# An encoder layer on one core: modulation rows by DMA, ring slots reordered, first two tiles together, three weight loads ahead

## The chip, the core and the metric

One core of one Trainium2 chip runs the whole layer. The time is that of one execution on the device, in microseconds; smaller is better. The engines are TensorE (PE, with its weight loads as PEld), VectorE (DVE), ScalarE (ACT), GpSimd (POOL) and SyncE (SP), which issues most of the DMAs.

## The reference, cut to what matters

One layer over x of 512 tokens by 1024 channels, all in float32. The part that the change touches is the first lines:

```python
mod = silu(c) @ w_ada + b_ada                     # (1, 6 * 1024)
sh1, sc1, gt1, sh2, sc2, gt2 = split(mod, 6)
h = rmsnorm(x, norm_mix_pre) * (1.0 + sc1) + sh1
z = h @ w_in                                      # (512, 1024) @ (1024, 4864)
zc, zr, zg = split(z, [1024, 1024 + 1792])        # conv, rwkv, gate columns
u = zc[:, :512] * sigmoid(zc[:, 512:])            # then a causal 31-tap depthwise convolution
...
zr = zr + (shifted(zr) - zr) * mu                 # then lora products, the RWKV-7 recurrence, heads normed
y = (g_conv * (silu(ln(conv)) @ p_conv) + g_rwkv * (rwkv @ p_rwkv)) @ w_o
x = x + gt1 * rmsnorm(y, norm_mix_post)
... a mixture of 64 experts follows, under sh2, sc2 and gt2
```

## The kernel before, in words

The kernel is a row of stages, each a block in which every engine runs its own written-out list of instructions; semaphores tie the lists together, and no planner moves anything. `project` makes mod and z, `rwkv` the recurrence, `merge_route` joins the two branches and chooses the experts, `experts` and `combine` do the rest.

`project` streams its weights through a ring of three slots of 2 MB (`ring`), in the order of the list STREAM: the 12 column slices of w_ada ("ada", 512 columns each) and the 10 slices of w_in ("in"). SyncE issues each load when the item three places before it in that list is done with: for an ada slice this is its sum on TensorE (s_adam), for an in slice the last z tile made from it (s_z).

An ada slice i becomes one row of mod, spread over all 128 partitions, in this way. VectorE sums silu(c)[k] times the eight 128-row pieces of the slice into `ada_acc` (`ada_partial`, L459, one instruction a piece, each waiting for the one before). For the first four slices TensorE takes two of the eight pieces itself (`ada_direct`, DIRECT = 2). TensorE then adds over the partitions with a matmul by ones (`ada_sum`, L373) and adds the bias row with a second matmul, by a column of the identity against `wide`, the 20 rows of b_ada and of the four norm gains (L374). Where the row is a scale or a gate, a third matmul (`gain_row`, L354) spreads the gain's row, ScalarE copies it to mod (`gain_copy`, L297), and VectorE multiplies it in (`mod_row`, L474). Slices 0 to 3 give sh1 and sc1, which h needs, and so come before h; slices 4 to 11 are used in later stages only, and are made one by one between the z tiles: the partial after the first tile of in slice s (VectorE), the three matmuls after its fourth tile (TensorE), for s from 1 to 8.

z comes in 38 tiles of 128 columns by 512 tokens. The product is made from exact halves: ScalarE rounds a pair of tiles' weights to `w_hi` (`split`, L310), GpSimd subtracts that from the weights into `ring_lo` (L269), h likewise is h_hi (ScalarE, L315) and h_lo (VectorE, L494 and L497), and a tile is 24 matmuls (L429), three for each of eight pieces k. Three PSUM banks rotate: ScalarE takes each tile, and for the 14 rwkv tiles VectorE adds the shifted part (L519) before the bank is free. Tiles 0 to 7 are the conv columns, 8 to 19 rwkv, 20 to 35 gates, 36 and 37 rwkv again. From tile 9 on VectorE also makes the 124 taps of the convolution (L506 and L510), six behind a tile, on the tiles that aren't the first of their slice.

`rwkv` begins with loads of the lora weights w2, a2 and g2 (L673 to L675) and with the products from them (L882). `merge_route` begins with loads of p_conv and p_rwkv and others (L1389 on); GpSimd writes `headones`, a block matrix of ones by head (L1421), TensorE takes head means with it (L1528), and goes on with p_conv (L1546).

## Time and profile before

| | us |
|---|---|
| median of 3 runs | 1486.5 |
| lowest, highest | 1485.4, 1490.94 |
| the profiled execution's own time | 1488.43 |
| span in its profile | 1486.7 |
| TensorE busy in the span | 1351.9 (91%) |
| VectorE busy | 1046.8 (70%) |
| ScalarE busy | 613.1 (41%) |
| GpSimd busy | 347.0 (23%) |

Time in the profile is counted from the span's start. `project` covers about the first 305 us of it, `rwkv` the time to 501.5, the merge and the routing the time to about 700, the experts nearly all of the rest. A count behind a row (x7) says that neighbouring instructions of one line are merged; the bracket at a row's end is the idle time ahead of it on its engine and what ended it. A float32 matmul by `ones` or `headones` is counted as two. PEclk is the granted TensorE clock as a share of full speed, 2.4 GHz.

### The profile page before, as it was taken

To read this page: it belongs to the slowest core of one execution; us is meant where nothing else is said; L and a number is where in the kernel's file an instruction comes from. 1 tells how busy PE (TensorE), PEld (TensorE's weight loads), DVE (VectorE), ACT (ScalarE), POOL (GpSimd) and SP (SyncE) were. 2 spreads that over 40 slices of the span, in tenths; PEclk is the share of its full clock that TensorE was granted. 3 is DMA by queue.
4 is the path that set the end of the run, shared out by engine and by line. 5 is a ranking of instruction groups with operands and counts; after the bars stand their busy time and mean duration, and the time that the engine had idled before them with its cause. 6 is when DMAs were issued, how large, how long until landed. Compare 5 with 4: busy or idle time off the path is not lost. (4 is left out here: it accounts for less than half of the span.)

```text
span 1486.7 us, 18817 instructions
## 1 busy us (share of the span) xinstructions
PE 1351.9 (91%) x5795; PEld 926.4 (62%) x5795; DVE 1046.8 (70%) x1651; ACT 613.1 (41%) x931; POOL 347.0 (23%) x350
## 2 busy tenths in 40 slices
PE   5799999974889799996899999999999999999947
PEld 3577677632779444443676776767767677676713
DVE  4539999968753253363688888888888888888617
ACT  3322212134224211212465655656656566565502
POOL 0243424233000000001222232322323223232200
PEclk9799999887789899998899999999999999999969
DMA  8434443210000461133599999999999999998358
GB/s 303 153 135 149 177 163 114 85 71 0 2 1 1 193 240 77 64 142 152 222 342 357 344 357 353 359 344 349 376 393 358 347 344 354 355 355 293 133 221 351
DMA packets 85266, 339.26 MB, mean 228 GB/s; under 512 B 16918, under 2 KB 20176, under 8 KB 58084
## 3 DMA queue, kind: packets, MB, share of 16 engines
q1 hardware_dynamic: 65400, 304.97, 54.5%
q0 software_dynamic: 19584, 33.60, 6.2%
q8 instruction: 27, 0.44, 0.1%
q14 instruction: 19, 0.16, 0.0%
q10 hardware_dynamic: 236, 0.09, 0.0%
HBM read 332.31 MB, written 44.04 MB: 253 GB/s over the span
## 5 line engine op out<-in xcount | busy, mean ns | idle before, releaser
L2158 DVE TENSOR_TENSOR gate_up_low<-gate_up,gate_up_high 128x1024 fp32r<-128x1024 f32 x204 | 244.7, 1220 | 42.2 <-ACT gate_up_high L2049 42.2
L2130 PE MATMUL py<-down_ring,hT 128*128 128x512 f32 x544 | 250.0, 602 | 0.9 <-ACT hT L2068 0.9
L2091 PE MATMUL p_gate_up<-gate_up_high,x_hi 128*128 128x512 f32 x544 | 242.7, 446 | 5.3 <-DVE x_lo L2167 5.3
L2091 PE MATMUL p_gate_up<-gate_up_low,x_hi 128*128 128x512 f32 x544 | 217.1, 399 | 0.0
L2091 PE MATMUL p_gate_up<-gate_up_high,x_lo 128*128 128x512 f32 x544 | 215.9, 397 | 0.0
L2049 ACT ACTIVATE gate_up_high<-gate_up 128x1024 fp32r<-128x1024 f32 x204 | 203.7, 1051 | 0.6 <-PEq L1308 0.6
L2130 PEld LDWEIGHTS py<-down_ring,hT 128*128 128x128 f32 x544 | 98.0, 190 | 98.8 <-issue 98.7
L2020 POOL TENSOR_TENSOR carrier<-offsets 1x1 f32<-1x1 f32 x136 | 29.2, 215 | 522.1 <-DVE tokens L2176 475.2
L269 POOL TENSOR_TENSOR ring_lo<-ring,w_hi 128x2048 fp32r<-128x2048 f32 x19 | 91.5, 4814 | 179.3 <-ACT w_hi L310 179.3
L2091 PEld LDWEIGHTS p_gate_up<-gate_up_high,x_hi 128*128 128x128 f32 x544 | 104.1, 191 | 45.1 <-issue 21.4
L429 PE MATMUL pz<-h_hi,w_hi 128*128 128x512 f32 x304 | 123.4, 406 | 7.7 <-DVE h_lo L497 7.7
L2091 PEld LDWEIGHTS p_gate_up<-gate_up_high,x_lo 128*128 128x128 f32 x544 | 103.8, 191 | 29.9 <-issue 10.8
L429 PE MATMUL pz<-h_lo,w_hi 128*128 128x512 f32 x304 | 122.1, 402 | 0.0
L429 PE MATMUL pz<-h_hi,ring_lo 128*128 128x512 f32 x304 | 122.1, 402 | 0.0
L2091 PEld LDWEIGHTS p_gate_up<-gate_up_low,x_hi 128*128 128x128 f32 x544 | 103.0, 189 | 24.2
L2036 POOL DMA_INDIRECT expert_rows<-y,row_ids x68 | 112.9, 1660 | 19.9 <-issue 19.9
L2073 ACT ACTIVATE y<-py 128x512 f32<-128x512 f32 x68 | 40.7, 599 | 179.4 <-PE py L2130 179.4
L510 DVE SCALAR_TENSOR_TENSOR co<-upad,taps,co 128x512 f32<-128x512 f32 x120 | 104.3, 936 | 0.0
L2158 DVE TENSOR_TENSOR gate_up_low<-x_again,gate_up_high 128x1024 fp32r<-128x1024 f32 x68 | 82.5, 1233 | 19.4 <-ACT gate_up_high L2049 19.4
L2062 ACT ACTIVATE x_hi<-px 128x512 fp32r<-128x512 f32 x136 | 73.9, 595 | 41.7 <-PE px L2104 41.7
L2167 DVE TENSOR_TENSOR x_lo<-px,x_hi 128x512 fp32r<-128x512 f32 x136 | 87.1, 682 | 4.1 <-ACT x_hi L2062 4.1
L459 DVE SCALAR_TENSOR_TENSOR ada_acc<-ring,silu_c,ada_acc 128x512 f32<-128x512 f32 x76 | 78.3, 1030 | 2.7
(359 smaller groups left out, 2038.2 us busy)
## 6 DMA issues: line engine op xcount, KB each, us to landing
down_ring<-in_we_down SPq DMA_DIRECT2D x68, 1024.0 KB, 9.6
gate_up<-in_we_gate SPq DMA_DIRECT2D x51, 1024.0 KB, 7.0
gate_up<-in_we_up SPq DMA_DIRECT2D x51, 1024.0 KB, 9.8
ring<-in_w_ada SPq DMA_DIRECT2D x12, 2048.0 KB, 7.9
ring<-in_w_in SPq DMA_DIRECT2D x9, 2048.0 KB, 10.1
x_again<-in_we_gate SPq DMA_DIRECT2D x17, 1024.0 KB, 7.0
x_again<-in_we_up SPq DMA_DIRECT2D x17, 1024.0 KB, 9.8
rows<-expert_rows SPq DMA_DIRECT2D x6, 2048.0 KB, 18.3
```

The source lines that it names most:

```text
L269: pool.tensor_tensor(pair(ring_lo, b), pair(ring, b), exact(w_hi[:, b % 2, :, :]), ALU.subtract).then_inc(s_wlo, 1)
L429: last = pe.matmul(pz[n % 3][:, :], weights, h[:, k, :], start=(k == 0 and i == 0), stop=(k == KD - 1 and i == 2))
L459: last = nc.vector.scalar_tensor_tensor(out=acc[:, i % 2, :], in0=ring[:, slot, k, :], scalar=c_k, in1=acc[:, i % 2, :], op0=ALU.mult, op1 ...
L510: done[r] = link.sign(nc.vector.scalar_tensor_tensor(out=mix.co[:, r, :], in0=u, scalar=tap, in1=mix.co[:, r, :], op0=ALU.mult, op1=ALU.add))
L2036: pool.indirect_dma_start(moe.rows, bass.IndirectOffsetOnAxis(row_ids[:, u % 4, 0:1], 0), y[:, u % 2, :], None, bounds_check=last_row, oob ...
L2049: act.activation(w_hi[:, u % 2, :, piece(i), :], moe.gate_up[u % RING][:, :, piece(i), :], ACT.Copy).then_inc(s_hi, 1)
L2062: act.activation(x_hi[:, u % 2, 4 * half:4 * half + 4, :], px[half][:, :].rearrange("p (k s) -> p k s", k=4), ACT.Copy).then_inc(s_xhi, 1)
L2073: act.activation(y[:, u % 2, 0:N], py[0][:, :], ACT.Copy).then_inc(s_yA, 1)
L2091: mm = pe.matmul(pgu[u % 2][:, :], x[:, u % 2, k, :], weights, start=(k == 0 and n == 0), stop=(k == KD - 1 and n == 2))
L2130: mm = pe.matmul(py[half][:, :], hT[:, u % 2, k, :], weights[:, k, half * N:half * N + N], start=(k == 0), stop=(k == 1))
L2158: V.tensor_tensor(moe.low[u % RING][:, :, piece(i), :], moe.gate_up[u % RING][:, :, piece(i), :], exact(w_hi[:, u % 2, :, piece(i), :]), A ...
L2167: V.tensor_tensor(x_lo[:, u % 2, ks, :], px[half][:, :].rearrange("p (k s) -> p k s", k=4), exact(x_hi[:, u % 2, ks, :]), ALU.subtract).th ...
```

## The change

- `wide` holds only bias rows: four rows of b_ada for slices 0 to 3, loaded by ScalarE's queue, and then a cleared tile of 128 rows (GpSimd's memset, behind the sum of slice 3, and ahead of its first `ring_lo`) into whose row 0 the bias of each slice from 4 on is loaded. VectorE's first piece takes it in, so the sum of these slices is one matmul.
- The gain rows are spread by four DMAs of 512 KB from ScalarE's queue straight into mod; `gain_row` and `gain_copy` go.
- x is the first load of SyncE's queue; c and the bias go by ScalarE's. A slot that held an ada slice is free as soon as VectorE's partial and TensorE's direct pieces have read it, without the sum. STREAM names slots: ada 4, 5 and 6 follow each other in slot 2 behind in 0 and in 1; then in 2, ada 7, in 3, ada 8, in 4, ada 9, in 5, ada 10, in 6, ada 11, in 7, in 8, in 9. in 0 comes in two halves with a semaphore each.
- TensorE takes four pieces of ada 3 (DIRECT = 2, 2, 2, 4) and the order of its work ahead of h changes.
- z tiles 0 and 1 are made together, 48 matmuls, with those of `ring_lo` two pieces behind. The remainder of pair 1 is made by VectorE and not by GpSimd.
- Partials and sums: 4 right before and after tiles 0 and 1; 5 behind tiles 1 and 3; 6 behind tiles 4 and 6; 7 to 11 behind the first and fourth tile of in slices 2 to 6. The taps go on the other tiles from 9, and so end with tile 33, not 35.
- w2, a2 and g2 are loaded into `ada_acc` once all sums are made; `headones` lives through all three stages; p_conv is loaded during `rwkv`, once the last Z64 product is made, and not in the merge.

The diff, cut (left out: names of semaphores, the slices' places in memory, and the same buffer written as `conv_stat` in place of `conv_stat[:, :]`):

```diff
-STREAM = [("ada", i) for i in range(4)]
...
-STREAM_AT = {item: n for n, item in enumerate(STREAM)}
 RING1 = 3
+FIRST, EARLY = 4, 3
+STREAM = ([(("ada", 0), 0), (("ada", 1), 1), (("ada", 2), 2), (("ada", 3), 0), (("in", 0), 1), (("in", 1), 0)]
+          + [(("ada", FIRST + _i), 2) for _i in range(EARLY)])
+for _i in range(2, len(IN_SLICES)):
+    STREAM.append((("in", _i), 1 - _i % 2))
+    if FIRST + EARLY + _i - 2 < ADA:
+        STREAM.append((("ada", FIRST + EARLY + _i - 2), 2))
+SLOT = dict(STREAM)
+USE = {item: sum(s == slot for _, s in STREAM[:_n]) for _n, (item, slot) in enumerate(STREAM)}
+BEFORE_IT = {item: [i for i, s in STREAM[:_n] if s == slot][-1:] for _n, (item, slot) in enumerate(STREAM)}
 PAIR = 2 * P
-FIRST = 4
-DIRECT = 2
+DIRECT = (2, 2, 2, 4)
 Z_TILES = [(s, t) for s, (_, w) in enumerate(IN_SLICES) for t in range(w // P)]
...
             if kind == "ada":
-                engine.wait_ge(s_adam, i + 1)
+                engine.wait_ge(s_ada, i + 1)
+                if i < FIRST:
+                    engine.wait_ge(s_dir, i + 1)
...
+        PARTIAL_AT = {1: FIRST + 1, 4: FIRST + 2}
+        SUM_AFTER = {3: FIRST + 1, 6: FIRST + 2}
+        for i in range(FIRST + EARLY, ADA):
+            PARTIAL_AT[Z_TILES.index((i - FIRST - EARLY + 2, 0))] = i
+            SUM_AFTER[Z_TILES.index((i - FIRST - EARLY + 2, 3))] = i
+        ROW_AT = {n + 1: i for n, i in SUM_AFTER.items()}
...
             sp.dma_start(x[:, :, :], w["x"][0].rearrange("(t p) d -> p t d", p=P)).then_inc(s_x, 16)
...
+            for item, slot in STREAM:
+                kind, i = item
+                for earlier in BEFORE_IT[item]:
+                    free_wait(sp, earlier)
...
-                sp.dma_start(ring[:, n % RING1, :, 0:width],
-                             source[:, at:at + width].rearrange("(k p) n -> p k n", p=P)).then_inc(
-                                 s_slot[n % RING1], 16)
+                parts = ((0, PAIR, s_half), (PAIR, N, s_slot[slot])) if item == ("in", 0) else ((0, width, s_slot[slot]),)
+                for c0, c1, landed in parts:
+                    sp.dma_start(ring[:, slot, :, c0:c1],
+                                 source[:, at + c0:at + c1].rearrange("(k p) n -> p k n", p=P)).then_inc(landed, 16)
+                if kind == "ada" and i >= FIRST:
+                    if i == FIRST:
+                        sp.wait_ge(s_zero, 1)
+                    sp.dma_start(wide[0:1, :], w["b_ada"][0:1, i * N:(i + 1) * N]).then_inc(s_brow, 16)
+            sp.wait_ge(s_adam, ADA)
+            sp.dma_start(acc[0:LORA_W, 0, :], w["w2"][0]).then_inc(mix.s_w, 16)
+            sp.dma_start(acc[LORA_W:P, 0, :], w["a2"][0]).then_inc(mix.s_w, 16)
+            sp.dma_start(acc[:, 1, :], w["g2"][0]).then_inc(mix.s_w, 16)
         @block.gpsimd
...
+            pool.wait_ge(s_adam, FIRST)
+            pool.memset(wide[:, :], 0.0).then_inc(s_zero, 1)
             for b in range(len(Z_TILES) // 2):
+                if b == 1:
+                    continue
...
+            act.dma_start(crow[:, :], w["c"][0].rearrange("(r n) -> r n", n=P)).then_inc(s_crow, 16)
+            act.dma_start(wide[0:FIRST, :], w["b_ada"][0, 0:FIRST * N].rearrange("(r n) -> r n", n=N)).then_inc(s_wide, 16)
+            rows = (keep.mod[:, D:2 * D], keep.mod[:, 2 * D:3 * D], keep.mod[:, 4 * D:5 * D], keep.gate2[:, :])
+            def gain_rows(g):
+                row = w[GAINS[g]][0].rearrange("(a n) -> a n", a=1).to_broadcast([P, D])
+                act.dma_start(rows[g], row).then_inc(s_gains if g else s_gain, 16)
...
-            def gain_copy(i):
-                if has_gain(i):
-                    act.wait_ge(s_gain, gains_to(i) + 1)
-                    act.activation(mod_part(keep, i), pg[:, :], ACT.Copy).then_inc(s_adag, 1)
...
+            gain_rows(0)
...
+            for g in range(1, len(GAINS)):
+                gain_rows(g)
...
+                if b == 0:
+                    act.wait_ge(s_half, 16)
+                else:
+                    slot_wait(act, ("in", Z_TILES[2 * b][0]))
...
-            def gain_row(i):
...
-                    pe.matmul(pg[:, :], keep.ident[0:N_WIDE, row:row + 1].to_broadcast([N_WIDE, P]),
-                              wide[:, :], start=True, stop=True).then_inc(s_gain, 1)
...
+                slot_wait(pe, ("ada", i))
+                for k in range(DIRECT[i]):
+                    mm = pe.matmul(out[:, :], keep.silu_c[:, k:k + 1].to_broadcast([P, P]), ring[:, SLOT[("ada", i)], k, :],
+                                   start=(k == 0), stop=False)
+                mm.then_inc(s_dir, 1)
...
+                mm = pe.matmul(out[:, :], keep.ones[:, :], acc[:, i % 2, :], start=(i >= FIRST), stop=(i >= FIRST))
...
-            def ada_sum(i):
-                out = pm[i % 2]
-                pe.wait_ge(s_ada, i + 1)
-                pe.matmul(out[:, :], keep.ones[:, :], acc[:, i % 2, :], start=(i >= FIRST), stop=False)
-                pe.matmul(out[:, :], keep.ident[0:N_WIDE, i:i + 1].to_broadcast([N_WIDE, P]), wide[:, :],
-                          start=False, stop=True).then_inc(s_adam, 1)
+                    mm = pe.matmul(out[:, :], keep.ident[0:FIRST, i:i + 1].to_broadcast([FIRST, P]), wide[0:FIRST, :],
+                                   start=False, stop=True)
+                mm.then_inc(s_adam, 1)
...
-            pe.wait_ge(s_wide, 16 * (1 + len(GAINS)))
-            gain_row(2)
+            pe.wait_ge(s_wide, 16)
...
+            ada_direct(1)
             ada_sum(0)
-            gain_row(3)
-            ada_direct(1)
             ada_sum(1)
             pe.wait_ge(s_hA, KD)
             mod_columns(0)
             pe.wait_ge(s_vrows, 16 * (len(VEC_ROWS) + 1))
             pe.transpose(pt[0][:, 0:N_VEC], vrows[:, :], keep.ident[0:N_VEC, 0:N_VEC])
             pe.transpose(pt[0][:, P:P + N_TAP], trows[:, :], keep.ident[0:N_TAP, 0:N_TAP]).then_inc(s_vecT, 1)
+            ada_direct(2)
+            ada_sum(2)
             mod_columns(1)
-            for i in (2, 3):
-                ada_direct(i)
-                ada_sum(i)
+            ada_direct(3)
+            ada_sum(3)
             mod_columns(2)
             mod_columns(3)
+            LAG = 2
+            for step in range(KD + LAG):
+                if step < KD:
+                    pe.wait_ge(s_hhi, step + 1)
+                    pe.wait_ge(s_hlo, step + 1)
+                    for n in range(2):
+                        weights = w_hi[:, 0, step, n * P:(n + 1) * P]
+                        pe.matmul(pz[n][:, :], weights, h_hi[:, step, :], start=(step == 0), stop=False)
+                        pe.matmul(pz[n][:, :], weights, h_lo[:, step, :], start=False, stop=False)
+                k = step - LAG
+                if k == 0:
+                    pe.wait_ge(s_wlo, 1)
+                if k >= 0:
+                    for n in range(2):
+                        last = pe.matmul(pz[n][:, :], pair(ring_lo, 0)[:, k, n * P:(n + 1) * P], h_hi[:, k, :],
+                                         start=False, stop=(k == KD - 1))
+                        if k == KD - 1:
+                            last.then_inc(s_z, 1)
+            ada_sum(FIRST)
             for n, (s, t) in enumerate(Z_TILES):
-                if t == 0:
-                    slot_wait(pe, ("in", s))
+                if n < 2:
+                    continue
                 if n >= 3:
                     pe.wait_ge(s_zA, n - 2)
...
-                pe.wait_ge(s_wlo, n // 2 + 1)
-                w_lo = pair(ring_lo, n // 2)
+                b = n // 2
+                if b == 1:
+                    pe.wait_ge(s_wlo1, 1)
+                else:
+                    pe.wait_ge(s_wlo, b)
+                w_lo = pair(ring_lo, b)
...
                         last = pe.matmul(pz[n % 3][:, :], weights, h[:, k, :],
                                          start=(k == 0 and i == 0), stop=(k == KD - 1 and i == 2))
                 last.then_inc(s_z, 1)
-                if t == 3 and 1 <= s <= ADA - 4:
-                    gain_row(s + 3)
-                    ada_direct(s + 3)
-                    ada_sum(s + 3)
+                if n in SUM_AFTER:
+                    ada_sum(SUM_AFTER[n])
         @block.vector
...
+                        last = nc.vector.scalar_tensor_tensor(out=acc[:, i % 2, :], in0=ring[:, slot, k, :], scalar=c_k,
+                                                              in1=wide[:, :], op0=ALU.mult, op1=ALU.add)
+                    elif k == first:
                         last = nc.vector.tensor_scalar(acc[:, i % 2, :], ring[:, slot, k, :], c_k, None, ALU.mult)
                     else:
...
+            dve.wait_ge(s_whi, 2)
+            nc.vector.tensor_tensor(pair(ring_lo, 1), pair(ring, 1), exact(w_hi[:, 1, :, :]), ALU.subtract).then_inc(s_wlo1, 1)
+            ada_partial(FIRST)
...
-                if t == 0 and 1 <= s <= ADA - 4:
-                    ada_partial(s + 3)
-                elif t == 3 and 1 <= s <= ADA - 4:
-                    mod_row(s + 3)
+                if n == 2:
+                    mod_row(FIRST)
+                if n in ROW_AT:
+                    mod_row(ROW_AT[n])
+                if n in PARTIAL_AT:
+                    ada_partial(PARTIAL_AT[n])
                 if n + 1 == NZ_CONV:
                     dve.wait_ge(s_const, 5)
                     dve.wait_ge(s_glu, RT_)
-                elif n + 1 > NZ_CONV and t:
+                elif n + 1 > NZ_CONV and n not in PARTIAL_AT:
                     conv_taps(made, min(TAPS, made + TAPS_A_TILE))
                     made = min(TAPS, made + TAPS_A_TILE)
...
         @block.sync
         def _(sp):
-            sp.dma_start(loras[0:LORA_W, :], w["w2"][0]).then_inc(s_w, 16)
-            sp.dma_start(loras[LORA_W:P, :], w["a2"][0]).then_inc(s_w, 16)
-            sp.dma_start(g2[:, :], w["g2"][0]).then_inc(s_w, 16)
             sp.dma_start(mix.spilled, mix.gates[:, NZ_GATE // 2:, :]).then_inc(s_spill, 16)
             sp.wait_ge(s_spill, 16)
...
         @block.sync
         def _(sp):
-            sp.dma_start(p_conv[:, :, :], w["p_conv"][0].rearrange("(k p) n -> p k n", p=P)).then_inc(s_pc, 16)
...
         @block.gpsimd
         def _(pool):
-            pool.memset(headones[:, :], 0.0).then_inc(s_g, 1)
-            for q in range(2):
-                pool.wait_ge(s_g, 1 + q)
...
+            mix.headones = mm.sb("head_ones", [P, P])
+            mix.s_w = mm.sem("lora_weights_in")
...
+            mix.s_pc = mm.sem("p_conv_in")
+            with ExitStack() as ahead:
+                mix.p_conv = Memory(nc, ahead).sb("p_conv", [P, RT_, D])
...
-            mix.p_conv, mix.p_rwkv = mm.sb("p_conv", [P, RT_, D]), mm.sb("p_rwkv", [P, RT_, D])
-            mix.headones, mix.br = mm.sb("headones3", [P, P]), mm.sb("b_router", [P, NE])
+            mm.sb("p_conv_kept", [P, RT_, D])
+            mix.p_rwkv = mm.sb("p_rwkv", [P, RT_, D])
```

## Rows read from the trace of the kernel before

**Rows 1.** Windows by stage: busy time (count) of each engine, PEclk, DMA share, GB/s.

```profile
0.00:50.80 50.80, 31.49 (x103) 15.93 (x104) 24.67 (x39) 19.40 (x30) 6.53 (x11) 0.92 0.86 309
50.80:105.70 54.90, 51.41 (x199) 39.03 (x199) 25.56 (x26) 16.09 (x17) 19.00 (x5) 0.91 0.20 71
105.70:304.90 199.20, 194.49 (x759) 145.13 (x758) 187.23 (x201) 44.50 (x47) 67.96 (x14) 0.95 0.39 140
304.90:501.50 196.60, 146.86 (x1025) 121.82 (x1024) 125.35 (x195) 64.78 (x115) 30.22 (x28) 0.83 0.04 14
```

**Rows 2.** ScalarE's timeline: one tile of the projection taken.

```profile
290.70 0.60 ACT L336 ACTIVATE gates<-pz 128x512 f32<-128x512 f32 x1 [4.84 <-PE pz L429]
```

**Rows 3.** TensorE's timeline after tile 7: start, us, engine, line, operation.

```profile
102.53 1.12 PE L354 MATMUL pg<-wide,ident 20*128 20x512 f32 x2
103.58 1.13 PE L373 MATMUL pm<-ada_acc,ones 128*128 128x512 f32 x2
```

**Rows 4.** TensorE's timeline: the two sums that wait for VectorE.

```profile
179.62 2.02 PE L373 MATMUL pm<-ada_acc,ones 128*128 128x512 f32 x2 [2.83 <-DVE ada_acc L459]
...
261.86 2.04 PE L373 MATMUL pm<-ada_acc,ones 128*128 128x512 f32 x2 [1.82 <-DVE ada_acc L459]
```

**Rows 5.** Windows: the stretch after the second of these waits.

```profile
261.80:271.80 10.00, 9.94 (x18) 5.70 (x19) 10.00 (x9) 0.11 (x1) 4.27 (x1) 0.50 0.75 270
```

**Rows 6.** VectorE's timeline: sums of ada products, a tile's second part, taps.

```profile
88.94 5.48 DVE L459 SCALAR_TENSOR_TENSOR ada_acc<-ring,silu_c,ada_acc 128x512 f32<-128x512 f32 x7
...
141.13 9.70 DVE L459 SCALAR_TENSOR_TENSOR ada_acc<-ring,silu_c,ada_acc 128x512 f32<-128x512 f32 x7
...
163.89 0.74 DVE L519 SCALAR_TENSOR_TENSOR zr<-pz,vec,zr 128x511 f32<-128x511 f32 x1
...
207.67 12.33 DVE L510 SCALAR_TENSOR_TENSOR co<-upad,taps,co 128x512 f32<-128x512 f32 x12
...
288.53 8.03 DVE L510 SCALAR_TENSOR_TENSOR co<-upad,taps,co 128x512 f32<-128x512 f32 x12
```

**Rows 7.** GpSimd's timeline: two weight remainders.

```profile
45.16 4.51 POOL L269 TENSOR_TENSOR ring_lo<-ring,w_hi 128x2048 fp32r<-128x2048 f32 x1 [28.62 <-ACT w_hi L310]
...
144.62 4.88 POOL L269 TENSOR_TENSOR ring_lo<-ring,w_hi 128x2048 fp32r<-128x2048 f32 x1 [8.44 <-ACT w_hi L310]
```

**Rows 8.** Timeline of SyncE's queue, ScalarE, TensorE and VectorE before the first tile.

```profile
2.87 0.41 SPq L243 DMA_DIRECT2D x<-in_x  x1
...
10.93 1.06 ACT L286 ACTIVATE hT<-x 128x1024 f32<-128x1024 f32 x1 [4.16 <-DMA x<-in_x]
...
26.48 1.02 PE L373 MATMUL pm<-ada_acc,ones 128*128 128x512 f32 x2
...
46.65 0.17 DVE L489 COPY modcol<-pt 128x16 f32<-128x16 f32 x1 [1.14 <-PE pt L381]
...
47.81 2.13 DVE L494 TENSOR_SCALAR hT<-hT,modcol 128x512 f32<-128x512 f32 x1 [0.98 <-ACT h_hi L315]
...
54.71 4.89 DVE L497 TENSOR_TENSOR h_lo<-hT,h_hi 128x512 fp32r<-128x512 f32 x1
...
61.89 0.54 DVE L494 TENSOR_SCALAR hT<-hT,modcol 128x512 f32<-128x512 f32 x1
62.46 0.69 DVE L497 TENSOR_TENSOR h_lo<-hT,h_hi 128x512 fp32r<-128x512 f32 x1
```

**Rows 9.** The page's DMA issues: count, KB each, median us to landing.

```profile
ring<-in_w_ada SPq DMA_DIRECT2D x12, 2048.0 KB, 7.9
```

**Rows 10.** ScalarE's and TensorE's timeline at the start of the RWKV stage.

```profile
307.27 0.61 ACT L728 ACTIVATE zr<-zr 128x512 f32<-128x512 f32 x1
...
311.17 7.19 PE L882 MATMUL all_banks<-zr,loras 64*128 64x512 f32 x8 [6.24 <-DMA g<-in_g]
```

**Rows 11.** TensorE's timeline at the start of the merge stage.

```profile
502.16 6.25 PE L1528 MATMUL c<-zr,headones 128*128 128x512 f32 x8 [3.78 <-POOL headones L1424]
510.47 8.83 PE L1546 MATMUL c<-co,p_conv 128*128 128x512 f32 x16 [2.06 <-DMA p_conv<-in_p_conv]
```

More of the change, by code:

```diff
@@ L361, in ada_direct @@
                     pe.wait_ge(s_mod, i - 1)
-                if i < FIRST:
-                    slot_wait(pe, ("ada", i))
-                    slot = STREAM_AT[("ada", i)] % RING1
-                    for k in range(DIRECT):
-                        pe.matmul(out[:, :], keep.silu_c[:, k:k + 1].to_broadcast([P, P]), ring[:, slot, k, :],
-                                  start=(k == 0), stop=False)
+                slot_wait(pe, ("ada", i))
[3 more added lines that the diff above has]
+                mm.then_inc(s_dir, 1)
             def ada_sum(i):
                 out = pm[i % 2]
+                if i >= FIRST:
+                    pe.wait_ge(s_mod, i - 1)
                 pe.wait_ge(s_ada, i + 1)
-                pe.matmul(out[:, :], keep.ones[:, :], acc[:, i % 2, :], start=(i >= FIRST), stop=False)
-                pe.matmul(out[:, :], keep.ident[0:N_WIDE, i:i + 1].to_broadcast([N_WIDE, P]), wide[:, :],
-                          start=False, stop=True).then_inc(s_adam, 1)
+                mm = pe.matmul(out[:, :], keep.ones[:, :], acc[:, i % 2, :], start=(i >= FIRST), stop=(i >= FIRST))
+                if i < FIRST:
+                    mm = pe.matmul(out[:, :], keep.ident[0:FIRST, i:i + 1].to_broadcast([FIRST, P]), wide[0:FIRST, :],
+                                   start=False, stop=True)
+                mm.then_inc(s_adam, 1)
             def mod_columns(i):
@@ L451, in ada_partial @@
                     dve.wait_ge(s_adam, i - 1)
-                slot = STREAM_AT[("ada", i)] % RING1
-                first = DIRECT if i < FIRST else 0
+                slot = SLOT[("ada", i)]
+                first = DIRECT[i] if i < FIRST else 0
                 for k in range(first, KD):
                     c_k = keep.silu_c[:, k:k + 1]
-                    if k == first:
+                    if i >= FIRST and k == 0:
+                        dve.wait_ge(s_brow, 16 * (i - FIRST + 1))
+                        last = nc.vector.scalar_tensor_tensor(out=acc[:, i % 2, :], in0=ring[:, slot, k, :], scalar=c_k,
+                                                              in1=wide[:, :], op0=ALU.mult, op1=ALU.add)
+                    elif k == first:
                         last = nc.vector.tensor_scalar(acc[:, i % 2, :], ring[:, slot, k, :], c_k, None, ALU.mult)
@@ L1525, in _ @@
         def _(pe):
-            pe.wait_ge(s_g, 3)
             for r in range(RT_):
```

104 lines of the change are left out of this document (39 added, 65 removed).

## The prediction, before any run of the change

> **What bounds the kernel now.** I first cut the span at the stages' borders [rows 1]. The change lies in the first three stretches and at the heads of two later ones; of the experts nothing is touched, so what is saved ahead of them should move the end by as much. Up to 50.8 us no tile of z is begun. From 50.8 to 105.7 the conv tiles 0 to 7 are made: TensorE is busy 51.4 of 54.9 us but VectorE only 25.6. From 105.7 to 304.9 come tiles 8 to 37, and the reader should see there that two engines are full, TensorE with 194.5 and VectorE with 187.2 of 199.2 us. So a saving on one of them alone need not count. I then read a tile's price: ScalarE takes neighbouring tiles 0.60 + 4.84 = 5.44 us apart [rows 2], so 30 tiles are 163.2 us and 36 us of the stretch are something else. Three float32 matmuls stand between tiles 7 and 8, about 1.05 us each, 3.15 together [rows 3]. Twice the sum waits for VectorE's partial, 2.83 and 1.82 us [rows 4], and after such a wait the granted clock is 0.50, which is 1.2 GHz, for 10 us [rows 5].
>
> VectorE's rows say why it is full [rows 6, 7]. Seven pieces of an ada slice take 5.48 us, 0.77 apart, when GpSimd is still, and 9.70 when its 4.88 us remainder (at 144.62) falls among them; twelve taps take 8.03 or 12.33. So each of GpSimd's remainders costs VectorE about 4.0 to 4.3 us, as if one waited for the other. A pair of tiles is 10.9 us, and of it VectorE loses 4.2.
>
> **Part 1, up to tile 0.** x is issued at 2.87 us behind six small loads, and ScalarE waits 4.16 us for it, to 10.93 [rows 8]. The six issues take about as long as x's own 0.41 us each or a little less, so x can go at about 0.8, 2.1 us earlier. A gain copy of 0.6 us leaves ScalarE among the transposes. From the sum at 26.48 to `modcol` at 46.65 is TensorE's own chain, 20.2 us: one gain row goes (1.05), two direct matmuls for slice 3 come (2.1), and I take the net as +0.9 less half a microsecond for the DMA wait of slice 3 that goes, since its load no longer stands behind a sum. Sum: -2.1 -0.6 +0.4 = -2.3; with 2 MB of gain rows now in the same full stream (a 2 MB ada load takes 7.9 us in the median [rows 9]) I keep -1.5, between 0 and -3. Split in halves, in 0 is not late for it. GpSimd's first remainder now waits for the sum of slice 3, as late as before, and so still stands on VectorE's first step of h, which took 2.13 us in place of 0.54 [rows 8].
>
> **Part 2, tiles 0 and 1.** Before, the second remainder held VectorE's h_lo for 4.89 us in place of 0.69 [rows 8], and TensorE stood. That goes: GpSimd skips that pair, and VectorE makes it after the last h_lo, as one instruction of 2048 columns, by length four times 0.6 = 2.4 us. Tile 2 began at 105.7 - 3.15 - 6 x 5.44 = 69.9, so the two tiles took 19.1 us. Now they are 48 matmuls, four to six for each of VectorE's steps of about 1.2 us (0.54 + 0.69 [rows 8]), and at the low clock that is 1.7 to 2.6 us, so TensorE sets the pace. It starts at the low clock, after standing as before; I take 10 us of that [rows 5], at 0.43 a matmul (a little under twice the 5.44 / 24 = 0.227 of the full clock) for 23 of them, and 25 at 0.227: 15.7 us, so -3.4. Then the sum of slice 4, +1.05, with its partial (eight pieces, 6.2 us) ready about when the tiles end, say 0.5 late. Tile 2 starts 1.5 + 3.4 - 1.5 = 3.4 us earlier. Bounds: 0 if the low clock lasts through all 48 (20.5 us) and -5 if it lasts 6 us.
>
> **Part 3, tiles 2 to 7.** Two sums of one matmul (2.1) for one of three (3.15): -1.05. The price: ada 5 is issued only when partial 4 is done and ada 6 when partial 5 is, through the one slot 2; each is 7.9 us of load and 6.2 of VectorE, 14 us, and four tiles behind it take 21.8, so sum 5 comes within 1 us of its place and sum 6 in time. In 2 stands in SyncE's queue behind ada 6; it is needed some 20 us later. For a short wait and its clock I set 1 us. That gives 3.4 again; with so many short waits near each other I keep 3.0 us for tile 8, between 2 later and 6 earlier.
>
> **Part 4, tiles 8 to 37.** TensorE loses 5 sums' bias matmuls and 4 gain rows, and two whole sums move ahead: before, 7 sums with 19 matmuls (20.0 us), now 5 with 5 (5.3), so 14.7 us less. If only TensorE counted, this would be the gain. But VectorE's list sets it. Up to the end of partial 11, which TensorE needs behind tile 27: 12 second parts at 0.66 (7.9), 5 partials at 6.2 (31.0), 72 taps at 0.66 (47.5), 4 mod rows (2.4), and ten remainders of GpSimd at 3.9 (39), 127.8 in all, begun 6.5 us after tile 8: 134. TensorE's own list to there is 20 x 5.44 + 4.2 = 113, so it stands some 20 us, spread over the five sums and some second parts. Then the last sum (1.05) and ten tiles (54.4): 189.8. VectorE has 52 taps, a row and four remainders left, 52 us, just beside these ten tiles. The same reckoning by difference: two partials (5.9 each) and two rows (0.6 each) leave VectorE, five first steps grow by 0.3, so 199.2 - 13 + 1.5 = 187.7. I take 189.7, -9.5. What TensorE loses in low clock after its waits is mostly absorbed, because it would have stood at the next sum anyway; only that after the last one counts, and 0 to 4 us of it are in the range. Bounds: 187.5 (VectorE's sum with no wait) and 197.
>
> **Part 5, the two later heads.** TensorE waits for the lora weights until 311.17, 6.24 us; without that, it waits for ScalarE's sigmoid, done at 307.88 [rows 10]: -3.2. What follows is a chain through the same engines, so I let all of it through; if a memset of GpSimd is late next, 1 us is lost. In the merge TensorE stands until 502.16 for `headones` and 2.06 us for p_conv [rows 11]: -0.7 (the barrier opens at about 501.5) and -2.06, together -2.7. The p_conv load runs under the recurrence, where the 16 DMA engines are 4% busy [rows 1]. The chain of ScalarE and VectorE for y doesn't cover this, since it hangs on square sums that TensorE makes behind p_conv's first two tiles, and so moves along.
>
> **The sum.** -3.0 -9.5 -3.2 -2.7 = -18.4 against the profiled execution's own 1488.4, of which 1486.7 is span: 1470.0. That run stands 1.9 over the median of 1486.5, so the prediction is 1468.
>
> **A rule against the change.** TensorE's granted clock fell to 0.50 after idle times of 1.8 and 2.8 us [rows 4, 5], and this change trades filler matmuls for such idle times. The Trainium skill, "TensorE: Matmul & The Clock Gate", section "HAM oscillation — how this bites in real kernels", describes a kernel in which each group of matmuls starts cold after each wait, with the whole price paid again. That is rival C.
>
> **Rivals.**
> A. TensorE's matmuls count in full: if VectorE's loss to GpSimd shrinks, say because the two interleave otherwise, stage 4 gives up to 163.2 + 5.3 + 10 us of waits and clock = 178.5, -20.7, in all -30: 1457. For it: TensorE too was full. Against it: 127.8 us of VectorE's list, counted by rows.
> B. The front gives nothing: the gain rows' DMAs delay ada 3 and in 0, or the chain ada 4, 5, 6 through one slot makes sums 5 and 6 wait with a slow clock behind. Tile 8 starts as before, and tiles 8 to 37 gain 7.5 in place of 9.5 by more low clock; with the 5.9 of the two heads that is 13.4 less: 1473. For it: in 7.9 us of load plus 6.2 of partial there is almost no slack for sum 5.
> C. Slower: in stage 4 each of about seven waits is followed by 10 us at half clock, a loss of 4.7 us each (23 matmuls x 0.2). It decides from the point where this loss exceeds the wait of about 3 us it would have had next, and no step is then absorbed: 168.5 + 7 x 3 + 7 x 4.7 = 222.4, +23; with -8.9 elsewhere +14: 1501. Against it: when TensorE is late, VectorE is not, and the wait after which the clock would fall is gone.
> D. The loads ahead do nothing, because the heads of `rwkv` and the merge stay bound by the low clock and by ScalarE: 5.9 less, 1474.
>
> **Chances.** Forecast 0.60, A 0.10, B 0.17, C 0.05, D 0.08. The forecast's own range is 1462 to 1475; 1458 to 1478 takes in B and D and leaves out C and half of A. A difference of 0.5% (7.4 us) is about what a measurement of this kernel can tell from none: faster by more than it 0.89, within it 0.06 (the weak end of B, C half absorbed), slower 0.05.
>
> **What would show it.** x's first square at about 9 us; `modcol` near 45; no h_lo over 1 us after the first; tile 2 near 66.5 and tile 8 near 102.7; sums as one matmul; a wait of 2 to 4 us on VectorE before most of sums 7 to 11, with few idle gaps on VectorE up to tile 27, and `project` ending near 292; the first lora matmul within 3 us of the stage's start; p_conv's first matmul directly behind the head means. Sums 7 to 11 without a wait would mean A; a granted clock near 0.5 through most of tiles 8 to 27 and gaps on VectorE, C; tile 8 at 105 or later, B.

## The result: 11 us instead of 18, and a stop of 12 us in the projection's tail

| | before | after |
|---|---|---|
| median of 6 runs each, one chip | 1489.15 us | 1478.03 us |
| lowest to highest | 1485.4 to 1490.94 | 1475.26 to 1481.02 |
| ratio, 95% interval | | 0.993 [0.9912, 0.9949] |
| the profiled execution's own time (span) | 1488.43 (1486.7) | 1480.75 (1479.0) |

The change makes the kernel faster, by 11.1 us on medians, where 18.4 were forecast. The median of 1478.03 lies 3 us above the forecast's own range (1462 to 1475) and just above the end of the wider one (1478). The changed kernel was timed twice more later, both times on one chip: 1474.93 (ratio 0.9923 [0.9904, 0.9942]) and 1476.17 (0.9928 [0.9902, 0.9954]). Its 18 executions go from 1474.1 to 1481.4, with their middle at 1476.4. The profiled execution above is one of the four slowest of them, which matters below.

In what follows a tile's time ("tile 8 at 104.2") is the moment at which TensorE begins it (the texts on record also say "taken"), except for the last tile, whose time is that at which ScalarE takes it. A remainder is one `ring_lo` subtract of GpSimd.

The first view is again that of the windows by stage, cut at the first tile, tile 8, the last tile taken, the merge's start and the gate product (us, busy time and count of each engine, PEclk, DMA share, GB/s):

```profile
0.00:49.30 49.30, 30.11 (x104) 16.33 (x104) 23.16 (x37) 18.82 (x28) 7.02 (x12) 0.92 0.97 351
49.30:104.20 54.90, 51.98 (x199) 40.88 (x200) 33.60 (x44) 13.16 (x14) 13.72 (x3) 0.89 0.51 184
104.20:307.20 203.00, 177.28 (x731) 141.34 (x729) 169.26 (x184) 44.51 (x44) 83.84 (x14) 0.93 0.32 112
307.20:501.20 194.00, 148.81 (x1024) 123.05 (x1024) 126.28 (x195) 64.75 (x115) 29.71 (x27) 0.82 0.06 22
501.20:536.80 35.60, 35.56 (x79) 15.69 (x80) 19.21 (x31) 9.81 (x14) 1.17 (x5) 0.95 0.79 303
```

Against [rows 1], the third stretch is the surprise. TensorE has 28 matmuls fewer and is busy 17 us less, VectorE is busy 18 us less, and yet the stretch takes 203.0 us in place of 199.2. GpSimd, with the same 14 remainders, is "busy" 83.8 in place of 68.0. By milestones the profiled pair divides like this (negative: the changed kernel is faster):

| stretch | forecast | profiled pair |
|---|---|---|
| up to tile 8 | -3.0 | -1.5 |
| tiles 8 to 37 | -9.5 | +3.8 |
| recurrence (with the lora head) | -3.2 | -2.5 |
| merge up to the gate product | -2.7 | -5.5 |
| rest (routing, experts) | 0 | -1.9 |

The group of waits of TensorE, 100 to 310 us (total, times, longest), names what held the third stretch, and the timelines of the three engines show it:

```profile
PE pz L458 <- POOL ring_lo L279: 12.3, 1, 12.3
PE pm L380 <- DVE ada_acc L490: 9.0, 4, 2.8
```

```profile
252.59 26.48 DVE L547 SCALAR_TENSOR_TENSOR co<-upad,taps,co 128x512 f32<-128x512 f32 x34
```

```profile
252.04 4.61 POOL L279 TENSOR_TENSOR ring_lo<-ring,w_hi 128x2048 fp32r<-128x2048 f32 x1 [11.78 <-ACT w_hi L327]
262.93 25.01 POOL L279 TENSOR_TENSOR ring_lo<-ring,w_hi 128x2048 fp32r<-128x2048 f32 x2 [6.28 <-ACT w_hi L327]
```

```profile
283.57 0.76 PE L458 MATMUL pz<-h_hi,w_hi 128*128 128x512 f32 x1 [12.28 <-POOL ring_lo L279]
```

VectorE runs 34 taps without a break, from 252.59 to 279.07. GpSimd's remainder of 262.93 (merged in the row with the next one) takes 20.5 us instead of some 4.6 and ends only 4.4 us after the last tap; TensorE stands 12.3 us for it and then works at half clock for 3.5 us. The windows of that stretch, of the changed kernel:

```profile
262.90:279.10 16.20, 8.39 (x37) 6.60 (x36) 16.17 (x25) 2.99 (x3) 16.17 (x1) 0.82 0.27 80
279.10:288.00 8.90, 4.43 (x13) 3.58 (x14) 0.00 (x0) 0.00 (x0) 8.84 (x2) 0.56 0.01 2
```

25 taps in 16.17 us are 0.65 us each, about the pace of free taps (0.67, [rows 6]): in those 16 us it is VectorE that loses nothing and GpSimd that gets nowhere, the reverse of the 4 us each that the prediction had charged to VectorE.

The table above is of one of the four slowest executions. The profile of x5 below, whose 1475.49 us lies near the median of the 18, divides otherwise against the same profile of before: +2.7 up to tile 8, -5.4 for tiles 8 to 37, -2.3 for the recurrence, -5.5 for the merge and -2.6 for the rest. There the larger miss is at the front.

### The profile page after: what moved, and what is told of

Read it like the earlier page. It is cut to its first block and busy times, and to the rows that moved or that the text cites. A ratio compares the mean times of both kernels' runs of the same rounds, so it can differ in the third digit from the quotient of the medians.

```text
span 1479.0 us, 18764 instructions
## 1 busy us (share of the span) xinstructions
PE 1332.5 (90%) x5767; PEld 924.7 (63%) x5767; DVE 1036.5 (70%) x1650; ACT 610.2 (41%) x923; POOL 358.1 (24%) x347
## 5 line engine op out<-in xcount | busy, mean ns | idle before, releaser
L279 POOL TENSOR_TENSOR ring_lo<-ring,w_hi 128x2048 fp32r<-128x2048 f32 x18 | 102.1, 5673 | 142.2 <-ACT w_hi L327 142.2
L458 PE MATMUL pz<-h_hi,w_hi 128*128 128x512 f32 x288 | 119.9, 416 | 16.7 <-POOL ring_lo L279 12.3
L458 PE MATMUL pz<-h_lo,w_hi 128*128 128x512 f32 x288 | 115.3, 400 | 0.0
L458 PE MATMUL pz<-h_hi,ring_lo 128*128 128x512 f32 x288 | 114.9, 399 | 0.0
L2139 PEld LDWEIGHTS px<-ident,xg 128*128 128x128 f32 x544 | 71.8, 192 | 13.0 <-DMA xg<-h_rows,tokens 6.7
```

The source lines that it names most:

```text
L279: pool.tensor_tensor(pair(ring_lo, b), pair(ring, b), exact(w_hi[:, b % 2, :, :]), ALU.subtract).then_inc(s_wlo, 1)
L458: last = pe.matmul(pz[n % 3][:, :], weights, h[:, k, :], start=(k == 0 and i == 0), stop=(k == KD - 1 and i == 2))
L2139: mm = pe.transpose(px[k // 4][:, (k % 4) * P:(k % 4 + 1) * P], rows[:, k, :], keep.ident[:, :])
```

## The experiments

**x1: VectorE gives way.** It waits for GpSimd's remainder ahead of the taps of tiles 29, 31 and 33.

```diff
+                    if n in (29, 31, 33):
+                        dve.wait_ge(s_wlo, n // 2 + 2)
                     conv_taps(made, min(TAPS, made + TAPS_A_TILE))
```

> The changed kernel, and VectorE waits ahead of the taps of tiles 29, 31 and 33 until GpSimd has made the weight remainders of pairs 16, 17 and 18. In the changed kernel's profile the remainder of pair 17 started at 262.93 us, stood beside VectorE's unbroken taps until these ended at 279.1 and was done at 283.4, and TensorE idled 12.28 us for it. Theory (a long unbroken run of taps keeps GpSimd from the ports that both use): no remainder over 6 us in this stage, no TensorE wait for one, last tile taken near 292.5 in place of 307.2, total 14 to 15 us less than the changed kernel, about 1463.5. Rival 1 (the delay is a chance of that one execution and mostly absent in the timed runs): total within 3 us of the changed kernel's 1478. Rival 2 (the waits only shift the loss, as VectorE has no slack here): TensorE ends the stage at 300 or later.

1471.67 us median, ratio 0.9904 [0.9873, 0.9935]. Up to tile 28 the profile is the changed kernel's to 0.1 us (104.2 and 237.2 against 104.2 and 237.1); then:

```profile
263.32 9.97 POOL L279 TENSOR_TENSOR ring_lo<-ring,w_hi 128x2048 fp32r<-128x2048 f32 x1 [6.27 <-ACT w_hi L327]
274.19 5.06 POOL L279 TENSOR_TENSOR ring_lo<-ring,w_hi 128x2048 fp32r<-128x2048 f32 x1 [0.91 <-ACT w_hi L327]
```

The long remainder is halved, TensorE waits 1.8 us for it and not 12.3, and the last tile is taken at 295.5 and not 307.2. The expectation was missed in size: it had no remainder over 6 us, the last tile near 292.5 and a total near 1463.5, 14 to 15 us less than the changed kernel. The total is 8.6 us under the changed kernel's profiled execution, which was one of its slowest, and 6.4 under its median. Tiles 8 to 37 take 191.3 us; the prediction's term was 189.7. So the taps ahead of which VectorE now waits cause the stop, and the term nearly holds without it.

**x2: no taps in the tail.** The taps of tiles 28 to 33 are left out of the computation.

```diff
+                elif 28 <= n <= 33:
+                    made = TAPS
```

> The changed kernel without the 34 taps of tiles 28 to 33 (left out: these terms of the convolution). If the taps beside GpSimd are the cause, GpSimd's remainders of pairs 17 and 18 take 4.6 us each, TensorE doesn't wait for them, and the last tile is taken near 291.5. If something else (a weight load, ScalarE's rounding) delayed pair 17, TensorE still waits some 12 us near 276 and the last tile is taken near 307.

1471.86 us. No remainder is waited for, as expected. The three remainders at 258.52, 269.40 and 280.28 take 4.60 us each, so VectorE's taps alone stretch them. The last tile comes at 299.6, though, where 291.5 was expected, and the reason lies earlier, at sum 11 (timelines of TensorE, then VectorE):

```profile
241.66 2.05 PE L380 MATMUL pm<-ada_acc,ones 128*128 128x512 f32 x2 [8.48 <-DVE ada_acc L490]
```

```profile
226.94 4.89 DVE L485 SCALAR_TENSOR_TENSOR ada_acc<-ring,silu_c,wide 128x512 f32<-128x512 f32 x1
231.87 9.64 DVE L490 SCALAR_TENSOR_TENSOR ada_acc<-ring,silu_c,ada_acc 128x512 f32<-128x512 f32 x7
```

Here two remainders, not one, fell into partial 11, which takes 14.5 us in place of some 6.2 without any. This execution runs the changed kernel's instructions up to there, with `modcol` 1.4 us later (46.50): the same instructions, begun a microsecond later, can make the other engine pay.

**x3: a breaker.** One column is copied from PSUM after the six taps of each of tiles 25 to 33.

```diff
+                    if 25 <= n <= 33:
+                        nc.vector.tensor_copy(crumb[:, n - 25:n - 24], pg[:, 0:1])
```

> The changed kernel with one tiny copy of a PSUM column on VectorE behind the six taps of each of tiles 25 to 33, on which nobody waits. Such an instruction has no SBUF input. Theory (GpSimd gets in where VectorE's run of two-input instructions is broken by one that has at most one SBUF input): each remainder gets in within about 4 us, takes under 9 us, TensorE waits 0 to 1 us for them, last tile taken near 292 to 294. Rival (GpSimd needs VectorE to be idle, or any gap between instructions will do and the copy leaves none): pair 17 is as late as in the changed kernel, last tile near 307.

1474.94 us, with no wait for a remainder. The last tile is taken at 301.2, where 292 to 294 was expected: tile 8 comes 3.1 us later than in the changed kernel's profile, and sum 11 waits 8.5 us as in x2. The timelines of VectorE and of GpSimd show how one that came between two taps got in:

```profile
268.87 4.05 DVE L548 SCALAR_TENSOR_TENSOR co<-upad,taps,co 128x512 f32<-128x512 f32 x6
272.84 0.14 DVE L576 COPY crumb<-pg 128x1 f32<-128x1 f32 x1
272.91 7.68 DVE L548 SCALAR_TENSOR_TENSOR co<-upad,taps,co 128x512 f32<-128x512 f32 x5
```

```profile
271.00 6.38 POOL L280 TENSOR_TENSOR ring_lo<-ring,w_hi 128x2048 fp32r<-128x2048 f32 x1 [5.99 <-ACT w_hi L328]
```

GpSimd asks at 271.00. The taps up to 272.84 run at their free pace; only the first after the crumb is long (five take 7.68 us, 4.4 more than 3.3), and the remainder is done at 277.38, 4.4 us after the crumb. So an instruction of VectorE that reads no two inputs from SBUF, even one of 0.14 us, was enough here to let GpSimd in. That it is needed is not shown, and other rows speak against it: in this profile a remainder that came at 281.88, 0.6 us after a crumb and long before the next, took only 5.22 us, and x5 below has one that got in at the next tap of an unbroken run.

In the kernel before, partial sums, mod rows and second parts of z [rows 6] stood between the taps, and none of its remainders took over 5.9 us. The change moved the partials ahead, and the taps of tiles 28 to 33 became one run. That this move made the long remainder possible is argued from the rows; no run puts the partials back between the taps.

The Trainium skill, "SBUF — State Buffer", section "Who interferes with whom", says that a VectorE instruction with two SBUF inputs contends with a GpSimd instruction that reads SBUF, and of VectorE's two-port modes that whoever issues first has the shared pair for the whole instruction. The trace agrees where a single instruction of VectorE waits out GpSimd's (the 4.9 us rows). It differs for the run of taps: those issued after GpSimd's 262.93 went ahead of it all the same.

**x4: only 4 of 124 taps.** Left out of the computation: the taps of k = 1 and above.

```diff
-                for product in range(first, end):
+                for product in range(first, min(end, RT_)):
```

> The changed kernel with only the first 4 of the 124 taps (left out: the rest of the convolution). It asks who sets the pace of tiles 8 to 37. Theory (VectorE's list does, as forecast): without some 80 us of taps TensorE waits for nothing there, and the stretch from tile 8 to the last tile, 203 us in the changed kernel, is 30 x 5.44 + 5 x 1.05 = 168.5, at most 173. Rival (TensorE's waits come from loads or from ScalarE): more than 180 us.

1452.22 us. Window of tiles 8 to 37:

```profile
108.60:276.40 167.80, 167.73 (x731) 136.82 (x729) 49.44 (x64) 44.44 (x45) 64.66 (x14) 1.00 0.39 135
```

TensorE is never idle and never slowed: 167.8 us is its own list, for which the prediction had 168.5. So 23 us of tiles 8 to 37 are VectorE's and GpSimd's doing even in x1, and rival A did not come about: VectorE's list sets this stage, as forecast.

**x5 and x9: the changed kernel again.** No edit.

> The changed kernel as it is, once more. If the long remainder of GpSimd beside VectorE's 34 unbroken taps (20.5 us where a free one takes 4.6) comes in every execution, the profile shows one remainder of 15 us or more after 255 us and the last tile taken at 305 to 308, and the median is near 1478. If it hangs on where in a tap GpSimd's request falls, the executions spread over some 10 us, and this profile may show the remainder at 5 to 10 us and the last tile taken near 293 to 298.

> The changed kernel as it is, beside the two below on the same chip. So far two profiled executions of this front showed a remainder of 20.5 us beside the 34 taps and two showed 8.0 and 9.4 us, and the tail from tile 28 to the last of z took 69.7 to 69.9 or 57.9 us. The theory (the port goes to whoever asks while it is free, so it hangs on where in a tap the request falls) expects a median of 1474 to 1479 again with a spread of 5 us or more, and a tail of one of the two lengths.

1474.93 (1474.08 to 1480.68) and 1476.17 (1474.5 to 1481.35). The profiled execution of x9 is the first one's twin: tile 8 at 104.2, a remainder of 20.5 us, last tile at 307.2. That of x5, at 1475.49, took another path; these are its rows of TensorE, VectorE and GpSimd:

```profile
70.55 2.04 PE L380 MATMUL pm<-ada_acc,ones 128*128 128x512 f32 x2 [8.04 <-DVE ada_acc L490]
...
291.15 0.47 PE L458 MATMUL pz<-h_hi,w_hi 128*128 128x512 f32 x1 [1.22 <-POOL ring_lo L279]
```

```profile
60.81 9.59 DVE L490 SCALAR_TENSOR_TENSOR ada_acc<-ring,silu_c,ada_acc 128x512 f32<-128x512 f32 x7
```

```profile
65.35 4.50 POOL L279 TENSOR_TENSOR ring_lo<-ring,w_hi 128x2048 fp32r<-128x2048 f32 x1 [16.74 <-ACT w_hi L327]
...
259.77 7.98 POOL L279 TENSOR_TENSOR ring_lo<-ring,w_hi 128x2048 fp32r<-128x2048 f32 x1 [18.30 <-ACT w_hi L327]
...
281.57 9.43 POOL L279 TENSOR_TENSOR ring_lo<-ring,w_hi 128x2048 fp32r<-128x2048 f32 x1 [6.16 <-ACT w_hi L327]
```

GpSimd got in before the last piece of partial 4, so sum 4 waited 8.0 us and not 2.9, and tile 8 was begun at 108.4. Sum 11 waited 8.5. But the tail, from tile 28 to the start of the last matmul of z, took 57.9 us and not 69.7. Six profiles have this tail unchanged (three of the changed kernel, and x7, x8 and x12 below): it is 69.7 to 69.9 us long in three and 57.9 in three. The three long ones are those in which sum 11 had waited only 2.7 to 2.8 us, the three short ones those in which it had waited 8.2 to 8.5.

The rows show how the two are tied. In each of the six a remainder comes beside the taps of tile 29 and stands. In the short tails TensorE is late by its wait, so VectorE catches up with the tiles: ahead of its first tap of tile 30 it has to wait for ScalarE to take that tile, 0.07 us in x5, 0.16 in x7 and 0.35 in x12, and in that pause GpSimd gets in. VectorE's timeline of x12:

```profile
263.40 22.93 DVE L540 SCALAR_TENSOR_TENSOR co<-upad,taps,co 128x512 f32<-128x512 f32 x22 [0.35 <-ACT gates L351]
```

In the changed kernel's first profile ScalarE took tile 30 at 255.0, and VectorE came to its taps some 9 us later and made no pause. But an unbroken run does not always keep GpSimd out. In x5 the next remainder came between two taps of that same run and got in at the next one, with no pause:

```profile
270.65 4.77 POOL L279 TENSOR_TENSOR ring_lo<-ring,w_hi 128x2048 fp32r<-128x2048 f32 x1 [2.90 <-ACT w_hi L327]
```

Why it got in at once, and the remainder of 262.93 only behind the last of 25 taps, no run shows.

The changed kernel's four executions at 1480.7 to 1481.4 have the lowest granted clock of its 18 (0.943 to 0.946); the two of them that were profiled hold the 20.5 us, and I take the other two for the same.

**x6: sums 4, 5 and 6 later**, behind tiles 2, 4 and 7, and the yields of x1.

```diff
-        SUM_AFTER = {3: FIRST + 1, 6: FIRST + 2}
+        SUM_AFTER = {2: FIRST, 4: FIRST + 1, 7: FIRST + 2}
```

> VectorE waits for GpSimd's remainder ahead of the taps of tiles 29, 31 and 33, and the sums of slices 4, 5 and 6 are moved behind tiles 2, 4 and 7. Theory: sum 4 no longer waits for its partial (2.9 us in the changed kernel) and the low clock behind that wait goes with it, so tile 8 is taken some 4 us earlier; with the tail at 1468.9 of span as in the first experiment, the span comes to 1464 to 1466. Rival: TensorE then waits as long at the later sums or for the eviction of tile 4, and the span stays at 1468 to 1470.

1475.55 (1474.95 to 1477.13), with a span of 1473.2 where the theory had 1464 to 1466 and the rival 1468 to 1470. The rival held, and worse. Tile 2 was begun at 64.5 and tile 4 at 76.3, 2.5 and 4.8 us earlier than in the changed kernel, but sum 5 then waited 4.7 us for a partial that had met a remainder (9.88 us), ada 6's load stood behind it, and tile 8 came at 106.7.

**x7: the lora loads alone back** at the start of the recurrence. **x8: the p_conv load alone back** in the merge.

```diff
+            sp.dma_start(loras[0:LORA_W, :], w["w2"][0]).then_inc(s_w, 16)
+            sp.dma_start(loras[LORA_W:P, :], w["a2"][0]).then_inc(s_w, 16)
+            sp.dma_start(g2, w["g2"][0]).then_inc(s_w, 16)
```

> The loads of w2, a2 and g2 alone go back to the start of the recurrence's part. Theory: the first sigmoid of the low-rank projections comes 6.5 us after that part's first DMA as in the kernel before, where the changed kernel has 2.8; the part is 2.5 to 3.2 us longer than the changed kernel's 192.2. Rival (the load was hidden, the 2.5 us came from the weights' place or from the clock): the part stays within 0.5 us of 192.2.

```diff
+            sp.dma_start(p_conv[:, :, :], w["p_conv"][0].rearrange("(k p) n -> p k n", p=P)).then_inc(s_pc, 16)
```

> The load of p_conv alone goes back to the start of the merge; the head-ones row stays loaded ahead. Theory: the 16 passes of p_conv wait for it and for the clock after that, and the time from the merge's first DMA to the gate product is 2.5 to 4.5 us longer than the changed kernel's 35.6. Rival: the head-ones row alone held the merge up, and the time stays within 0.5 us of 35.6.

Read by the parts they touch, since their fronts and tails differ as above. x7: that part takes 196.0 us against 192.2 (190.3 to 192.5 in the other profiles with the load ahead). x8: up to the gate product 39.8 us against 35.6 (35.4 to 36.8 in the others with the load ahead). TensorE's timelines at these places, of the changed kernel and then of x7 and x8:

```profile
310.27 3.19 PE L923 MATMUL all_banks<-zr,ada_acc 64*128 64x512 f32 x4 [3.10 <-ACT zr L769]
...
501.24 5.37 PE L1563 MATMUL c<-zr,head_ones 128*128 128x512 f32 x8 [3.32 <-PEq L89]
506.44 7.03 PE L1581 MATMUL c<-co,p_conv 128*128 128x512 f32 x16
```

```profile
309.48 7.19 PE L923 MATMUL all_banks<-zr,ada_acc 64*128 64x512 f32 x8 [6.20 <-DMA ada_acc<-in_g]
```

```profile
514.52 8.78 PE L1581 MATMUL c<-co,p_conv 128*128 128x512 f32 x16 [2.34 <-DMA p_conv<-in_p_conv]
```

The lora loads are worth 3.8 us (3.2 forecast). p_conv is worth 4.2: the wait of 2.34 and 1.75 of slow clock behind it (8.78 against 7.03), which the prediction had left out. What is left of the merge's 5.5 lies at the head means: begun 0.6 us earlier after the merge's first DMA, and 5.37 long against 6.25 [rows 11].

**x10 and x11: x1 again, and GpSimd kept out of two partials.** x10 is x1; x11 adds:

```diff
                 pool.wait_ge(s_whi, b + 1)
+                if b == 2:
+                    pool.wait_ge(s_ada, FIRST + 1)
+                if b == 15:
+                    pool.wait_ge(s_ada, ADA)
```

> The first experiment's kernel (VectorE waits for GpSimd's remainder ahead of the taps of tiles 29, 31 and 33), once more beside the changed kernel. Theory: the tail takes 57.9 us in each execution, so the slow end of the spread is cut off: median 1471 to 1475, 2 to 5 us under the changed kernel's on the same chip. Rival: its 1471.7 was this chip's or a lucky phase, and the two medians agree within 1.5 us.

> As x10, and GpSimd waits for partial 4 ahead of the remainder of tiles 4 and 5, and for partial 11 ahead of that of tiles 30 and 31. Theory: sum 4 waits about 3 us in every execution and never 8, partial 11 holds at most one remainder and sum 11 waits at most 4 us and never 8.5; tile 2 is taken 21.9 to 22.1 us after modcol, tiles 8 to 37 take 189 to 191 us, and the median is 1469 to 1471.5. Rival: the lock only moves to the next piece, partial or tap, and the median is that of x10.

On one chip, with x9: x9 1476.17 (1474.5 to 1481.35), x10 1474.87 (1470.12 to 1475.8), x11 1471.73 (1470.12 to 1475.27; ratio to before 0.99 [0.9873, 0.9927]). The yield moves the median only 1.3 us, within the 1.5 us that I had given its rival. It does cut off the slow end: of the 18 executions with it on this chip (x6, x10, x11) none is over 1477.2 us, of the changed kernel's 12 there (x5, x9) four are. With both, five of six executions lie below the fastest of x9; against x10 the intervals overlap, so what the keeping out adds to the yield is not clear of noise. In x11's profile sum 4 waits 3.8 us, the longest wait of sums 7 to 11 is 4.4 where it was 8.5 in x2, x3 and x5, and tiles 8 to 37 take 191.8 us, each a little over what I had expected. On this chip it is the fastest version with the whole computation, 4.4 us below the changed kernel.

**x12: the second remainder back to GpSimd**, alone.

```diff
-                if b == 1:
-                    continue
...
-            dve.wait_ge(s_whi, 2)
-            nc.vector.tensor_tensor(pair(ring_lo, 1), pair(ring, 1), exact(w_hi[:, 1, :, :]), ALU.subtract).then_inc(s_wlo1, 1)
```

> The changed kernel, but the second remainder (tiles 2 and 3) is GpSimd's again and not VectorE's. Theory (the prediction's part 2): it starts at about 54 us as in the kernel before and holds one h_lo or hT of VectorE for 4 to 4.9 us, TensorE's steps of tiles 0 and 1 behind it come as much later, and tile 2 is taken more than the 21.9 us after modcol that the changed kernel shows (26.2 where GpSimd fell in partial 4); about 24 to 25. Rival: the 2.3 us that VectorE saves, and GpSimd out of the way of partial 4, give it back, and tile 2 is taken 21 to 22 us after modcol.

VectorE, GpSimd and TensorE in tiles 0 and 1:

```profile
53.85 4.93 DVE L526 TENSOR_TENSOR h_lo<-hT,h_hi 128x512 fp32r<-128x512 f32 x1
```

```profile
53.45 4.78 POOL L277 TENSOR_TENSOR ring_lo<-ring,w_hi 128x2048 fp32r<-128x2048 f32 x1 [4.65 <-ACT w_hi L325]
```

```profile
58.92 0.47 PE L426 MATMUL pz<-h_hi,w_hi 128*128 128x512 f32 x1 [2.52 <-DVE h_lo L526]
```

The 4.9 us `h_lo` of [rows 8] is back, and tile 2 is begun 23.6 us after `modcol`. The changed kernel shows 21.9 when GpSimd misses partial 4 and 26.2 when it doesn't (x5). By these single profiles the move is worth 1.7 us, where the prediction counted on most of 3.4, and it ends in a place where it can lose 2.6.

## Why the prediction was too low

**Up to tile 0: as forecast, but not told from the spread.** The first square starts at 8.90, `modcol` at 45.10 (forecast 9 and 45). In the 13 profiles with this code it lies between 44.08 and 46.89, so 1.5 us is no more than its spread.

**Tiles 0 to 7: a gain that came and was lost again.** From tile 0 to tile 8 it takes 54.9 us, as in the kernel before, where 1.5 less was forecast. The h_lo are all 0.69 us again, and the low clock of tile 0 lasts 5.3 us and not 10. The new wait is where I had allowed 1 us, behind tile 1 (TensorE, of the changed kernel):

```profile
65.95 2.04 PE L380 MATMUL pm<-ada_acc,ones 128*128 128x512 f32 x2 [2.92 <-DVE ada_acc L490]
```

It costs 2.9 us, with some 5 us at half clock behind it. I had priced sums 5 and 6 closely and not asked when partial 4 could be done: it stands behind VectorE's 2.28 us remainder and ends at 65.8, while TensorE is through with tile 1 at 62.9. Tile 8 came at 104.2, between forecast (102.7) and rival B (105 or later); in others it came at 107 to 110, from the waits at sums 4 and 5. In x5 it is the wait of 8.0 us at sum 4, for which the sum had 0.5, that turns 3.0 earlier into 2.7 later: in the executions near the median this is the term with the largest error.

**Tiles 8 to 37: the failed step.** The list up to the end of partial 11 held: 131.6 us after tile 8 for my 134, sums waiting 1.4 to 2.8 us, VectorE without a gap from its first tap on, TensorE's own list 167.8 for 168.5. What failed is the sentence on the last ten tiles, that beside VectorE's taps there they take their 54.4 us. I had charged every meeting of the two engines to VectorE, at 3.9 us, with rows in front of me in which the runs of taps were short [rows 6]. The reordering itself removed what broke them up. In the profiled execution that costs 12.3 us of standing, and tiles 8 to 37 take 203.0 for 189.7. In the others, as x5, they take 193.9. There the list up to sum 11 took 134.5 us, as forecast in spite of the wait of 8.5, and the 4.2 too many lie behind it: tile 28 is made at half clock for its first part and costs some 2.4 us more (ScalarE takes it 7.8 us after its start), and the wait of 1.2 us for the remainder of 281.57 makes tile 36 1.5 us longer. The prediction had allowed 0 to 4 us of low clock there in its range, and none in its sum.

**The heads: right in kind, the merge too small** by the clock behind the wait, 1.75 us, which I had counted in other places and not in this one. This hid a part of the miss: without its 2.8 us, and the 1.9 of the untouched rest, the profiled pair would show 3 us in place of 7.7.

**Rivals.** A (TensorE's matmuls count in full) is excluded by x4 against x1, C (clock swinging through the sums) by a mean clock of 0.93 in a stretch that holds a 12 us stop, D by x7 and x8. B described the front in seven of the ten profiles that have it unchanged (tile 8 at 105 or later), with sum 4 as the place and not sums 5 and 6 alone. The mechanism that decided, an engine kept waiting by unbroken work on its neighbour, was in none of them.

**Open.** I did not find what sets the phase: `modcol` varies by 2.8 us among the 13 profiles, and with it the side on which each remainder falls. Nor is it known why some remainders get in at the next tap and others not at all. That the unprofiled executions split as the profiled do rests on their times and clocks alone.

## What to carry to other kernels

When two engines share a lock, count for each meeting who pays and when the loser gets in: a cost read where runs are short (4 us on VectorE) can turn into one on the other engine (16 us on GpSimd) where the runs are long. Moving short work of another kind out of a stretch is not only a saving; ask what it had been breaking up. And when one profile disagrees with the median's neighbours, look at a second and third execution before explaining the first: here the same instructions took two paths 6 us apart.

## What the hardware showed that I had not expected

- A GpSimd subtract of 128x2048 that takes 4.6 us took 20.5 beside 25 back-to-back taps of VectorE, each reading two tensors from SBUF. It did so in two of the three profiles of the changed kernel, and in x8.
- A VectorE copy of one column from PSUM (0.14 us, x3) was enough to let it in, and so was a pause of 0.07 us (x5). In the same run of taps another remainder got in with neither.
- TensorE's clock fell to its half level behind idle times of 2.3 us (x8: 16 passes 8.78 us for 7.03) and 2.9 us (changed kernel, sum 4: two passes 2.04 us), and in the kernel before behind 1.8 [rows 4]. Behind 1.4 us (changed kernel, sum 7) the granted clock stayed at 1.00. In x11 sum 4 waited 3.8 us and took only 1.36, because the clock fell while it ran: it was 0.70 from 65 to 67 us and 0.50 from 67 to 69.
